# A hybrid decoder layer: router weights loaded earlier, and half of the output projection of two token tiles placed around the last head sums

## The chip, the cores and the metric

The kernel runs on one core of a Trainium2 chip. The core has four compute engines that work side by side and meet at semaphores: TensorE (PE in the profile), VectorE (DVE), ScalarE (ACT) and GpSimd (POOL). A fifth, SyncE (SP), only issues DMA transfers here. The metric is the time of one execution on the device in microseconds (us); the shown time is the median of three runs.

## What is computed

One layer over 1024 tokens with 1024 features, all in float32:

```python
h = rmsnorm(x, ln1_g)
p = h @ w_in                                  # columns shared out to two kinds of heads
oA = stick_breaking_attention(q, k, v)        # 8 heads of 64, features 0..511
oB = gla_chunked(q, k, v, log_a)              # 4 heads, 128 values each, features 512..1023
oB = rmsnorm(oB per head, gla_norm_g) * silu(g_r)
x1 = x + concat(oA, oB) @ w_out
h2 = rmsnorm(x1, ln2_g)
logits = h2 @ [w_group, w_expert] + [b_group, b_expert]    # 4 + 32 columns
y  = x1 + top-2 experts of the best group, each (silu(h2 @ gate) * (h2 @ up)) @ down
out = rmsnorm(y, ln_f_g)
```

Every large product is made exact to float32 by splitting both factors into a high part (float32r, written by ACT) and the rest (written by DVE): three matmuls, high x high, rest x high and high x rest.

## The kernel before

The program is a row of blocks; within a block each engine has its own list of instructions, in an order written by hand, and at the end of a block all engines meet. The blocks are: norm and transposition of x, stick-breaking attention, linear attention (`linear_attention`, L661), output projection and routing (`mix_and_route`, L1362), the experts, and the combination. TensorE's products write to eight banks of PSUM (`bank(k, i)`), and each engine that reads a bank frees it for the next product.

**Linear attention** works on two pairs of heads, p = 0 and 1. TensorE's list interleaves twenty projections `project(n)` (24 matmuls of 512 columns each, L1171) with the seven levels of each pair's scores (`level(g)`, L1247, small matmuls in plain float32). DVE puts a level's result into the score tile with `place_level(g)` (L1027). For pair 1, `turn_v(1)` (L1187) transposes the values, token tiles two at a time, n = 0 to 3, into banks 2 and 3 by turns; so n = 2 waits until DVE's `take_v(1)` (L940) has copied n = 0 away, and in DVE's list `take_v(1)` stands behind `place_level(7)`. In TensorE's list it stands behind `level(7)`.

The pair ends so: `level(12)`, `level(13)`, then `outputs(1)` (L1260, L1265), which needs every level placed; DVE's `gate_out(1)` (L1036) reads the output from banks 0 to 3 and ACT squares it; `sums(1, h)` (L1274) adds the squares over a head's 128 features by a matmul with ones, into banks 4 to 7; ACT takes logarithm and exponential (L835, L839), DVE multiplies (`normed`, L1043), and the block ends. Meanwhile the rows of `w_out` arrive and are split by ACT (L846) and DVE (`split_wo(kd)`, L1047), one of eight row blocks kd at a time, in the space that the projections have left. The features 0 to 511 of the concatenation, `cat[:, 0:4]`, come from stick-breaking and are complete long before. So for token tile 0 their half of the output projection, 24 matmuls (L1326), stands at the end of this block, behind the sums, into banks 0 and 1. DVE's `split_wo(0)` and `split_wo(1)` stand ahead of `place_level(12)` and `place_level(13)`.

**Output projection and routing** goes over eight token tiles t. On TensorE: two column halves of 24 matmuls (L1773), 12 each for t = 0, whose first half is done; between the halves the eight transpositions of tile t - 1 (`turn`, L1743); behind them the router's product of tile t - 1 (`score`, L1753). A tile's matmuls wait for its split parts (`in_hi`, ACT L1539; `in_lo`, DVE L1664). DVE adds x to the product (L1671, tile `cat`), ACT squares and takes the root (L1545, L1549), DVE inverts (L1636), normalizes (L1650), splits the tile after next, and copies the transposed tile (L1629) for the router. Both lists are in strict order.

SP's list in this block begins with two tiles of x and `g2`, then the router's gains, weights and biases (L1445 to L1449: `g2c`, `wr`, `rb`), then a blank list to DRAM (`slots`, L1451), then the first expert's gate and up weights, four transfers of 1024 KB (L1456). DVE waits for all six small loads at t = 0, ahead of the splitting of tile 1, and multiplies the router's weights by the gains (L1660).

Of the kernel before, what the change touches and what calls it, by code (L numbers as in the profile page):

```python
# [99 lines left out]
def _build(nc, ctx, a):  # L100
# [51 lines left out]
    with ExitStack() as c0:  # L152
# [11 lines left out]
        with ExitStack() as front:  # L164
# [6 lines left out]
            w.update(w2=sb("w2", [P, KW], F32, front), gb=sb("gb", [P, GLA_PAIRS], F32, front),  # L171
                     gn=sb("gn", [P, GLA_HEADS], F32, front), small=sem("g_small"))
            with ExitStack() as c2:
                norm_and_turn(k, c2, h_hi, h_lo, cat, w)
            with ExitStack() as c2:
                stick_breaking(k, c2, h_hi, h_lo, cat, w)
            with ExitStack() as c2:
                linear_attention(k, c2, h_hi, h_lo, cat, w, wo)
        passing[0] = False
        gf, gf_in = sb("gf", [P, D], F32, c0), sem("c_gf")  # L180
        with ExitStack() as c:
            tiles = expert_tiles(k, c, cat, raw, high, lower)
            with ExitStack() as c2:
                tables = mix_and_route(k, c2, c, cat, in_parts, tiles, wo, retire)
            x1_in = experts(k, c, tables, tiles, cat, in_parts, gf, gf_in)
# [475 lines left out]
def linear_attention(k, c, h_hi, h_lo, cat, w, wo):  # L661
# [47 lines left out]
    def sum_banks(p, h):  # L709
        return ps[:, 4 * p + 2 * h:4 * p + 2 * h + 2, :]  # L710
# [7 lines left out]
    with nc.Block() as block:  # L718
        @block.sync
        def _(sp):  # L720
            for t in range(first + 2, LAST):
                sp.wait_ge(lo_done, t - 2)
                sp.dma_start(w_raw[:, t % 3], w_dram[:, :, TILE_COLS[t]:TILE_COLS[t] + P]).then_inc(w_in_s[t % 3], 16)
            sp.wait_ge(lo_done, LAST)
# [48 lines left out]
        def _(act):  # L773
# [131 lines left out]
            act.activation(w_hi[:, 0, 0:SB_PAIRS], cat[:, 0:SB_PAIRS, 0:P], ACT.Copy).then_inc(cathi, 1)  # L905
# [13 lines left out]
        def _(dve):  # L919
# [15 lines left out]
            def take_v(p):  # L935
                if p:
                    dve.wait_ge(o_ready, p)
                for n in range(4):
# [128 lines left out]
            take_v(0)  # L1067
# [42 lines left out]
            exponents(9)  # L1110
            place_level(7)
            take_v(1)
# [37 lines left out]
        def _(pe):  # L1150
# [24 lines left out]
            def turn_v(p):  # L1175
                pe.wait_ge(out_done, 16 if p else 4)
# [4 lines left out]
                for n in range(4):  # L1181
# [94 lines left out]

            pe.wait_ge(small, 48)
# [6 lines left out]
            turn_v(0)  # L1284
# [16 lines left out]
            project(15)  # L1301
            level(7)
            turn_v(1)
# [14 lines left out]
            outputs(1)  # L1318
            for h in range(2):
                sums(1, h)  # L1320
            pe.wait_ge(catlo, 1)
            pe.wait_ge(wolo, SB_PAIRS)
            for hf in range(2):
                for kd in range(SB_PAIRS):
                    for m, (x_, w_) in enumerate(((w_hi, wo_hi), (w_lo, wo_hi), (w_hi, wo_lo))):
                        pe.matmul(bank(k, hf), x_[:, 0, kd, :], w_[kd][:, hf * HALF:(hf + 1) * HALF],  # L1326
                                  start=(kd == 0 and m == 0), stop=False)
# [36 lines left out]
def mix_and_route(k, c, out_c, cat, cat_parts, tiles, wo, retire):  # L1364
# [17 lines left out]
    g2c = sb("g2c", [P, KD], F32, c)  # L1382
    x1T = sb("x1T", [P, KD, P], F32, c)
    wr = sb("wr", [P, KD, LOGITS], F32, c)
    rb = sb("rb", [P, LOGITS], F32, c)
# [44 lines left out]

    def x1(t):
# [6 lines left out]
    with nc.Block(no_gpsimd_drain=True) as block:  # L1438
        @block.sync
        def _(sp):  # L1440
# [3 lines left out]
            with nc.allow_non_contiguous_dma(reason="a thousand gains, features to partitions"):  # L1444
                sp.dma_start(g2c[:], a["ln2_g"][0].rearrange("(k p) -> p k", p=P)).then_inc(small, 16)  # L1445
# [814 lines left out]
```

## Time and profile before

| | |
|---|---|
| median of 3 runs | 1294.22 us (1292.25 to 1297.98) |
| the profiled execution | 1290.5 us |
| its span, first to last instruction | 1288.9 us |
| TensorE busy / VectorE / ScalarE / GpSimd | 93% / 70% / 57% / 24% |
| linear attention | to 516.6 us of the span |
| output projection and routing | from there; the first expert matmul starts at 663.7 us |
| experts and combination | the rest |

All places in the text are microseconds from the start of the span. A row of a timeline gives the start of an instruction (or of a merged run of equal ones), its duration, the engine and the line, what is written and read, and in brackets how long the engine was idle before it and who ended that wait. TensorE's matmuls overlap in the pipeline, so that the start of the next one tells more than the end of the last. The granted clock is 1.00 at 2.4 GHz and 0.50 at 1.2 GHz.

### The profile page before, as it was taken

What the parts mean: (1) busy time and instruction counts of PE and PEld (TensorE: products, weight loads), DVE (VectorE), ACT (ScalarE), POOL (GpSimd) and SP (SyncE); (2) the same over time, 40 slices, a digit from 0 to 9 for tenths busy, and PEclk for the clock granted to TensorE, in tenths of its full rate; (3) what the DMA queues carried; (4) which work ended last, traced back from release to release, by engine and by line L of the source; (5) the groups of instructions that cost most, each with busy time, mean ns of one, the idle gap of its engine ahead of it and who ended that gap; (6) DMA issues with size and microseconds to landing.
All of it is one profiled execution on the core that took longest, in us unless ns stands there. A gap on an engine that the chain in (4) does not pass through costs nothing. (4 is left out here: it accounts for less than half of the span.)

```text
span 1288.9 us, 18150 instructions
## 1 busy us (share of the span) xinstructions
PE 1193.2 (93%) x6596; PEld 903.0 (70%) x6596; DVE 902.0 (70%) x844; ACT 739.0 (57%) x760; POOL 307.7 (24%) x273
## 2 busy tenths in 40 slices
PE   3999999999999998799649999999999999999975
PEld 2777777877788786688536777777777777777742
DVE  3366656565475476344759989988989989899725
ACT  5365556464442426211428788777787777887613
POOL 1000000000211010100442444455444454444400
PEclk8999999999999998899869999999999999999988
DMA  5210101000210021833169999999999999999757
GB/s 179 66 34 17 34 18 34 18 17 1 71 45 17 1 99 33 273 126 98 61 239 405 395 382 386 381 388 386 383 380 384 383 387 386 381 386 385 281 198 293
DMA packets 83152, 271.63 MB, mean 211 GB/s; under 512 B 14640, under 2 KB 45472, under 8 KB 58528
## 3 DMA queue, kind: packets, MB, share of 16 engines
q1 hardware_dynamic: 72640, 248.31, 51.7%
q0 software_dynamic: 9312, 18.45, 4.4%
q10 hardware_dynamic: 1152, 4.19, 0.8%
q8 instruction: 34, 0.56, 0.2%
q14 instruction: 14, 0.11, 0.0%
HBM read 253.91 MB, written 25.79 MB: 217 GB/s over the span
## 5 line engine op out<-in xcount | busy, mean ns | idle before, releaser
L2089 PE MATMUL ps<-w_high,in_hi 128*96 128x512 f32 x512 | 204.1, 399 | 4.8 <-DVE hid L2017 2.9
L2089 PE MATMUL ps<-w_lower,in_hi 128*96 128x512 f32 x512 | 202.3, 395 | 0.0
L2089 PE MATMUL ps<-w_high,in_lo 128*96 128x512 f32 x512 | 201.8, 394 | 0.0
L1359 POOL DMA_INDIRECT x_g<-h_dram,who x33 | 157.8, 4781 | 39.7 <-POOL who L1355 27.8
L2031 DVE TENSOR_TENSOR d_lo<-cat,d_hi 128x2048 fp32r<-128x2048 f32 x64 | 146.2, 2286 | 24.6 <-ACT d_hi L1953 24.6
L2003 DVE TENSOR_TENSOR w_lower<-w_raw,w_high 128x2048 fp32r<-128x2048 f32 x62 | 141.7, 2285 | 24.6 <-ACT w_high L1932 24.6
L2008 DVE TENSOR_TENSOR w_lower<-w_raw,w_high 128x2048 fp32r<-128x2048 f32 x64 | 143.4, 2279 | 4.0 <-PEq L1438 4.0
L1938 ACT ACTIVATE w_high<-w_raw 128x2048 fp32r<-128x2048 f32 x62 | 118.9, 1919 | 24.3 <-PE ps L2089 24.3
L1953 ACT ACTIVATE d_hi<-cat 128x2048 fp32r<-128x2048 f32 x64 | 122.3, 1912 | 16.5 <-PEq L1438 13.6
L1932 ACT ACTIVATE w_high<-w_raw 128x2048 fp32r<-128x2048 f32 x62 | 118.2, 1907 | 0.0
L510 DVE TENSOR_TENSOR_SCAN prod<-cat 128x256 f32<-128x256 f32 (+7 forms) x64 | 83.4, 1344 | 41.7 <-ACT cat L438 41.6
L2089 PEld LDWEIGHTS ps<-w_high,in_hi 128*96 128x96 f32 x512 | 83.4, 163 | 38.7 <-DVE w_lower L2003 3.4
L2089 PEld LDWEIGHTS ps<-w_lower,in_hi 128*96 128x96 f32 x512 | 83.2, 163 | 35.6
L2089 PEld LDWEIGHTS ps<-w_high,in_lo 128*96 128x96 f32 x512 | 83.5, 163 | 33.2 <-issue 0.8
L1874 POOL DMA_INDIRECT y_dram<-y,where x32 | 36.2, 1132 | 272.5 <-ACT y L1963 272.5
L577 PE MATMUL ps<-w_high,in_hi 128*128 128x512 f32 x232 | 93.9, 405 | 1.4 <-PEq L213 1.4
L577 PE MATMUL ps<-w_lower,in_hi 128*128 128x512 f32 x232 | 92.5, 399 | 0.0
L577 PE MATMUL ps<-w_high,in_lo 128*128 128x512 f32 x232 | 92.0, 396 | 0.0
L2116 PE MATMUL ps<-d_hi,hT_hi 128*96 128x512 f32 x256 | 81.0, 398 | 1.6 <-DVE hT_lo L2026 1.5
L2116 PE MATMUL ps<-d_lo,hT_hi 128*96 128x512 f32 x256 | 80.3, 395 | 0.0
L2116 PE MATMUL ps<-d_hi,hT_lo 128*96 128x512 f32 x256 | 80.3, 395 | 0.0
L742 POOL MEMSET kl<- 128x2048 f32 x1 | 1.8, 1804 | 281.7 <-POOLq L376 281.7
(315 smaller groups left out, 2382.4 us busy)
## 6 DMA issues: line engine op xcount, KB each, us to landing
w_raw<-exp_w_gate SPq DMA_DIRECT2D x64, 1024.0 KB, 10.1
w_raw<-exp_w_up SPq DMA_DIRECT2D x64, 1024.0 KB, 11.6
cat<-exp_w_down SPq DMA_DIRECT2D x64, 1024.0 KB, 10.8
w_raw<-w_in SPq DMA_DIRECT2D x22, 512.0 KB, 3.8
xt<-x SPq DMA_DIRECT2D x8, 512.0 KB, 6.8
w_raw<-w_out SPq DMA_DIRECT2D x8, 512.0 KB, 5.1
x_g<-x SPq DMA_DIRECT2D x8, 512.0 KB, 3.7
x_dram<-cat SPq DMA_DIRECT2D x8, 512.0 KB, 4.9
```

Of the source, the lines that this page charges most:

```text
L510: dve.tensor_tensor_scan(prod[:, h, T - nk:T][:, ::-1], x, x, 1.0, ALU.mult, ALU.bypass)\
L577: mm = pe.matmul(out, w[:, t % 2, x // 3, :], h[:, x // 3, cols], start=(x == 0), stop=(x == 3 * KD - 1))
L1359: pool.indirect_dma_start(x_g[0:CAP, j, :], None, k["h2_dram"][:, :], bass.IndirectOffsetOnAxis(ap=who[j][0:CAP, 0:1], axis=0), bounds_che ...
L1874: pool.indirect_dma_start(k["y2_dram"][:, :], bass.IndirectOffsetOnAxis(ap=where[j][0:CAP, 0:1], axis=0), y[j][0:CAP, :], None, bounds_che ...
L1932: act.activation(g_hi[:, 4 * m:4 * m + 4], w_g[:, 4 * m:4 * m + 4], ACT.Copy).then_inc(ghi, 1)
L1938: act.activation(u_hi[:, 4 * m:4 * m + 4], w_u[:, 4 * m:4 * m + 4], ACT.Copy).then_inc(uhi, 1)
L1953: act.activation(d_hi[:, part], w_d[j][:, part], ACT.Copy).then_inc(dhi, 1)
L2003: dve.tensor_tensor(g_lo[:, part], w_g[:, part], g_hi[:, part].bitcast(F32), ALU.subtract).then_inc(glo, 1)
L2008: dve.tensor_tensor(u_lo[:, part], w_u[:, part], u_hi[:, part].bitcast(F32), ALU.subtract).then_inc(ulo, 1)
L2031: dve.tensor_tensor(d_lo[:, part], w_d[j][:, part], d_hi[:, part].bitcast(F32), ALU.subtract).then_inc(dlo, 1)
L2089: mm = pe.matmul(out, x_[:, n // 3, :], w_[:, n // 3, :], start=(n == 0), stop=(n == 3 * KD - 1))
L2116: mm = pe.matmul(ps[0:CAP, 2 + m, :], x_[:, f, :], w_[:, f, cols], start=(f == 0 and n == 0), stop=(f == KF - 1 and n == 2))
```

## The change

- The five router loads leave SP's list in `mix_and_route` and go into SP's list in `linear_attention`, behind the load of the sixth weight tile (t = first + 5). Their tiles live from there on, with a semaphore of their own. DVE's multiplication of the router's weights moves behind the addition of x at t = 0; `normalize(0)` gets a wait for `g2`.
- `turn_v(1)` and `take_v(1)` are cut in two. The first half (n = 0, 1) goes ahead of `level(7)` on TensorE and ahead of `place_level(7)` on DVE.
- DVE does `place_level(12)` first, then `split_wo(0)`, then `place_level(13)`, then `split_wo(1)` to `(3)`.
- The first half of the output projection is made for two token tiles: tile 0 into banks 4 and 5 between `outputs(1)` and `sums(1, h)`, tile 1 into banks 2 and 3 behind the sums. The sums go to banks 6, 7 and 0, 1. ACT and DVE split `cat[:, 0:4]` for both tiles. In `mix_and_route` tile 1 then has 24 matmuls instead of 48, and its split there covers the features 512 to 1023 only.

```diff
@@ linear_attention
     def sum_banks(p, h):
-        return ps[:, 4 * p + 2 * h:4 * p + 2 * h + 2, :]
+        first_bank = ((0, 2), (6, 0))[p][h]
+        return ps[:, first_bank:first_bank + 2, :]
@@ SP
                 sp.dma_start(w_raw[:, t % 3], w_dram[:, :, TILE_COLS[t]:TILE_COLS[t] + P]).then_inc(w_in_s[t % 3], 16)
+                if t == first + 5:
+                    with nc.allow_non_contiguous_dma(reason="a thousand gains, features to partitions"):
+                        sp.dma_start(g2c[:], a["ln2_g"][0].rearrange("(k p) -> p k", p=P)).then_inc(router_in, 16)
+                    sp.dma_start(wr[:, :, 0:GROUPS], a["w_group"][0].rearrange("(k p) n -> p k n", p=P)).then_inc(router_in, 16)
...
@@ ACT
-            act.activation(w_hi[:, 0, 0:SB_PAIRS], cat[:, 0:SB_PAIRS, 0:P], ACT.Copy).then_inc(cathi, 1)
+            for t in range(2):
+                act.activation(w_hi[:, t, 0:SB_PAIRS], cat[:, 0:SB_PAIRS, t * P:(t + 1) * P], ACT.Copy).then_inc(cathi, 1)
@@ DVE
             exponents(9)
+            take_v(1, 0, 2)
             place_level(7)
-            take_v(1)
+            take_v(1, 2, 4)
...
-            for kd in range(2):
+            place_level(12)
+            split_wo(0)
+            place_level(13)
+            for kd in range(1, SB_PAIRS):
                 split_wo(kd)
-            place_level(12)
-            place_level(13)
-            for kd in range(2, SB_PAIRS):
-                split_wo(kd)
-            dve.wait_ge(cathi, 1)
-            dve.tensor_tensor(w_lo[:, 0, 0:SB_PAIRS], cat[:, 0:SB_PAIRS, 0:P], w_hi[:, 0, 0:SB_PAIRS].bitcast(F32),
-                              ALU.subtract).then_inc(catlo, 1)
+            for t in range(2):
+                dve.wait_ge(cathi, t + 1)
+                dve.tensor_tensor(w_lo[:, t, 0:SB_PAIRS], cat[:, 0:SB_PAIRS, t * P:(t + 1) * P],
+                                  w_hi[:, t, 0:SB_PAIRS].bitcast(F32), ALU.subtract).then_inc(catlo, 1)
@@ PE
-            def turn_v(p):
-                pe.wait_ge(out_done, 16 if p else 4)
+            def turn_v(p, first, last):
+                pe.wait_ge(out_done, (16 if last == 4 else 15) if p else 4)
...
             project(15)
+            turn_v(1, 0, 2)
             level(7)
-            turn_v(1)
+            turn_v(1, 2, 4)
...
             outputs(1)
+            mix_first_half(0, 4)
             for h in range(2):
                 sums(1, h)
...
+            mix_first_half(1, 2)
@@ mix_and_route, DVE
-                if t == 0:
-                    dve.wait_ge(small, 96)
-                    dve.tensor_tensor(wr[:], wr[:], over(g2c[:], [P, KD, LOGITS]), ALU.mult).then_inc(ready, 1)
...
                 if t >= 1:
                     score(t - 1)
+                if t == 0:
+                    dve.wait_ge(router_in, 80)
+                    dve.tensor_tensor(wr[:], wr[:], over(g2c[:], [P, KD, LOGITS]), ALU.mult).then_inc(ready, 1)
                 if 0 <= t < NT - 1:
                     invert(t)
                     normalize(t)
@@ mix_and_route, PE
-                    n = 0 if t else 3 * SB_PAIRS
+                    n = 0 if t > 1 else 3 * SB_PAIRS
-                    for kd in range(0 if t else SB_PAIRS, KD if t < NT else 0):
+                    for kd in range(0 if t > 1 else SB_PAIRS, KD if t < NT else 0):
```

The new `mix_first_half(t, at)` waits for the split of tile t and for the rests of `w_out`'s first four row blocks, then issues the 24 matmuls that stood at L1326, into `bank(k, at + hf)`.

## Rows read from the trace of the kernel before

**Rows 1.** Timeline of PE, 445 to 452 us: start, duration, instruction, [idle before].

```profile
444.97 2.00 PE L1247 MATMUL ps<-ql,kl 64*128 64x64 f32 x32
446.90 1.09 PE L1187 MATMUL ps<-ident,cat 128*128 128x128 f32 x8
450.07 1.25 PE L1187 MATMUL ps<-ident,cat 128*128 128x128 f32 x8 [2.07 <-DVE gv L940]
451.07 0.47 PE L1171 MATMUL ps<-w_high,in_hi 128*128 128x512 f32 x1
```

**Rows 2.** Timeline of DVE at the same place.

```profile
447.02 2.47 DVE L1027 COPY_PREDICATED s_all<-masks,ps 128x512 f32<-128x512 int32 x2 [12.41 <-PE ps L1247]
```

**Rows 3.** Stretches: length, busy PE, PEld, DVE, ACT, POOL (x); clock; DMA share, GB/s.

```profile
452.00:491.40 39.40, 39.40 (x354) 34.01 (x352) 28.29 (x42) 10.27 (x14) 5.40 (x5) 1.00 0.30 108
...
492.90:499.60 6.70, 5.14 (x24) 5.14 (x25) 6.52 (x8) 6.67 (x7) 0.00 (x0) 0.50 0.00 0
...
506.60:509.80 3.20, 3.20 (x5) 1.35 (x4) 3.06 (x3) 1.11 (x1) 0.00 (x0) 0.50 0.00 0
510.00:515.90 5.90, 5.90 (x26) 4.50 (x24) 1.69 (x2) 4.41 (x4) 0.00 (x0) 1.00 0.00 0
...
527.10:533.70 6.60, 5.39 (x13) 4.23 (x14) 3.74 (x5) 3.67 (x5) 0.61 (x1) 0.50 1.01 376
...
700.00:1240.00 540.00, 537.75 (x2538) 387.02 (x2537) 476.07 (x299) 412.77 (x297) 240.80 (x178) 1.00 0.98 374
```

**Rows 4.** Timeline of PE: the first pair's outputs and second sum.

```profile
424.98 3.73 PE L1260 MATMUL ps<-s_all,gv 128*128 128x128 f32 x32
...
437.71 1.88 PE L1274 MATMUL ps<-b_all,ones 128*128 128x512 f32 x4
```

**Rows 5.** Timeline of PE, 487 to 545 us.

```profile
487.71 3.79 PE L1247 MATMUL ps<-ql,kl 64*128 64x64 f32 x64
494.46 6.31 PE L1260 MATMUL ps<-s_all,gv 128*128 128x128 f32 x32 [2.96 <-DVE s_all L1027]
...
505.18 5.40 PE L1274 MATMUL ps<-e,ones 128*128 128x512 f32 x8 [2.65 <-DVE cat L1036]
...
518.34 0.50 PE L1773 MATMUL ps<-w_high,in_hi 128*128 128x512 f32 x1 [2.30 <-DVE in_lo L1664]
...
528.31 0.80 PE L1773 MATMUL ps<-w_high,in_hi 128*128 128x512 f32 x1 [4.24 <-DVE in_lo L1664]
...
542.79 1.87 PE L1753 MATMUL ps<-wr,x1T 128*128 128x36 f32 x16
544.49 0.48 PE L1773 MATMUL ps<-w_high,in_hi 128*128 128x512 f32 x1
```

**Rows 6.** Timeline of DVE: placing and splitting around 490 us.

```profile
489.39 2.36 DVE L1047 TENSOR_TENSOR w_lower<-w_raw,w_high 128x1024 fp32r<-128x1024 f32 x2 [2.98 <-ACT w_high L846]
491.67 2.74 DVE L1027 COPY_PREDICATED s_all<-masks,ps 128x512 f32<-128x512 int32 x4
```

**Rows 7.** Timeline of DVE in the output projection, tiles 0 and 1.

```profile
526.67 0.46 DVE L1660 TENSOR_TENSOR wr<-wr,g2c 128x288 f32<-128x288 f32 x1 [8.38 <-DMA rb<-b_expert]
...
528.18 1.22 DVE L1671 TENSOR_TENSOR cat<-ps,x_g 128x1024 f32<-128x1024 f32 x1
...
534.33 1.22 DVE L1664 TENSOR_TENSOR in_lo<-cat,in_hi 128x1024 fp32r<-128x1024 f32 x1
537.07 1.29 DVE L1629 COPY x1T<-ps 128x512 f32<-128x512 f32 x2 [1.53 <-PE ps L1743]
```

**Rows 8.** Timeline of SP: weight tiles, router loads, blank list.

```profile
343.09 9.63 SPq L723 DMA_DIRECT2D w_raw<-w_in  x2
...
518.17 0.43 SPq L1445 DMA_DIRECT2D g2c<-ln_g  x1
...
524.24 0.43 SPq L1451 DMA_DIRECT2D slots<-h  x1
```

**Rows 9.** DMA issues, 516 to 530 us: KB, us to landing.

```profile
slots<-h SPq DMA_DIRECT2D x1, 576.0 KB, 3.8
```

More of the change, by code:

```diff
@@ L176, in _build @@
                 stick_breaking(k, c2, h_hi, h_lo, cat, w)
+            router = (sb("wr", [P, KD, LOGITS], F32, c0), sb("rb", [P, LOGITS], F32, c0), sb("g2c", [P, KD], F32, c0),
+                      nc.alloc_semaphore(name="router_in"))
             with ExitStack() as c2:
-                linear_attention(k, c2, h_hi, h_lo, cat, w, wo)
+                linear_attention(k, c2, h_hi, h_lo, cat, w, wo, router)
         passing[0] = False
@@ L183, in _build @@
             with ExitStack() as c2:
-                tables = mix_and_route(k, c2, c, cat, in_parts, tiles, wo, retire)
+                tables = mix_and_route(k, c2, c, cat, in_parts, tiles, wo, router, retire)
             x1_in = experts(k, c, tables, tiles, cat, in_parts, gf, gf_in)
@@ L657, in _, with linear_attention @@
                     turn_v(p)
-def linear_attention(k, c, h_hi, h_lo, cat, w, wo):
+def linear_attention(k, c, h_hi, h_lo, cat, w, wo, router):
     nc, sb, sem, ps, a, ident, ones, V, A, G = (
@@ L720, in _ @@
         def _(sp):
+            wr, rb, g2c, router_in = router
             for t in range(first + 2, LAST):
@@ L933, in gate_1, with take_v @@
                 dve.tensor_tensor(gate_place(1, h), gate_place(1, h), b_all[:, h], ALU.mult).then_inc(r_done, 1)
-            def take_v(p):
+            def take_v(p, first, last):
                 if p:
                     dve.wait_ge(o_ready, p)
-                for n in range(4):
+                for n in range(first, last):
                     dve.wait_ge(vturn, 4 * p + n + 1)
@@ L1066, in _ @@
             split_lo(first + 3)
-            take_v(0)
+            take_v(0, 0, 4)
             decayed(0)
@@ L1180, in turn_v @@
                     pe.wait_ge(x_done, 4)
-                for n in range(4):
+                for n in range(first, last):
                     if p and n >= 2:
@@ L1275, in sums, with mix_first_half @@
                 mm.then_inc(summed, 1)
+            def mix_first_half(t, at):
+                pe.wait_ge(catlo, t + 1)
+                pe.wait_ge(wolo, SB_PAIRS)
+                for hf in range(2):
+                    for kd in range(SB_PAIRS):
+                        for m, (x_, w_) in enumerate(((w_hi, wo_hi), (w_lo, wo_hi), (w_hi, wo_lo))):
+                            pe.matmul(bank(k, at + hf), x_[:, t, kd, :], w_[kd][:, hf * HALF:(hf + 1) * HALF],
+                                      start=(kd == 0 and m == 0), stop=False)
             pe.wait_ge(small, 48)
@@ L1361, in gather_rows, with mix_and_route @@
                             bounds_check=T - 1, oob_is_err=False).then_inc(gathered[j], 16)
-def mix_and_route(k, c, out_c, cat, cat_parts, tiles, wo, retire):
+def mix_and_route(k, c, out_c, cat, cat_parts, tiles, wo, router, retire):
     nc, sb, sem, ps, a, ident, ones, V, G = (k[n] for n in ("nc", "sb", "sem", "ps", "a", "ident", "ones", "V", "G"))
@@ L1381, in mix_and_route @@
     g2 = sb("g2", [P, D], F32, c)
[L1382 removed]
     x1T = sb("x1T", [P, KD, P], F32, c)
[L1384 to L1385 removed]
+    wr, rb, g2c, router_in = router
     logits = sb("logits", [P, NT, LOGITS], F32, c)
@@ L1647, in normalize @@
                     dve.wait_ge(blanked, 16)
+                    dve.wait_ge(small, 16)
                 if t >= 2:
@@ L1772, in _ @@
                         for x_, w_ in ((cat_hi, wo_hi), (cat_lo, wo_hi), (cat_hi, wo_lo)):
-                            mm = pe.matmul(bank(k, 2 * j + hf), x_[:, j, kd, :], w_[kd][:, cols], start=(n == 0),
+                            mm = pe.matmul(bank(k, mix_bank(t, hf)), x_[:, j, kd, :], w_[kd][:, cols], start=(n == 0),
                                            stop=(n == 3 * KD - 1))
```

33 lines of the change are left out of this document (14 added, 19 removed).

## The prediction, made before the change was built

> **What bounds the kernel now.** I read the page first. TensorE is busy nearly all the time, and the slices where it is not lie at the start, around 500 to 540 us, in the routing and at the end; in the same slices its granted clock falls. The experts, more than 500 us, are full: TensorE works 537.75 of 540 us, with the DMA engines at a share of 0.98 [rows 3]. Nothing of the change lies in there, so what is won ahead of them should arrive at the end as it is. Then I read TensorE's timeline from the last projections to tile 2, and for each idle time the timeline of the engine named in its bracket.
>
> From 452 to 491.4 us TensorE is never idle, while VectorE works 28.3 and ScalarE 10.3 of those 39.4 us [rows 3]: there TensorE is the limit. Ahead of it is an idle time of 2.07 us, in which it waits for VectorE to copy the turned values [rows 1]; VectorE is late with that only since its list has `place_level(7)` first, which waits 12.41 us for TensorE [rows 2]. Behind it TensorE waits four times: 2.96 us for the last placing, 2.65 us for the gated outputs, 2.30 us at the border of the blocks, 4.24 us for the split of tile 1 [rows 5]. The last one comes from the router's loads: VectorE stood 8.38 us waiting for them, with the split behind that wait [rows 7]. Three of these idle times are followed or accompanied by a granted clock of 0.50, that is 1.2 GHz: 492.9 to 499.6, 506.6 to 509.8 and 527.1 to 533.7 us [rows 3].
>
> **The values' transposition in two parts.** From `level(7)` to `project(16)` TensorE takes 451.07 - 444.97 = 6.10 us [rows 1]. With two turns ahead of the level, two behind, no wait is left: 1.93 us of level (446.90 - 444.97) and twice 1.09 us of turns make 4.1 us. What the first turns need from ScalarE and VectorE is there by then: VectorE is idle until 447.02 [rows 2] and copies n = 0 and 1 while the level runs. Moved instructions: sixteen matmuls and two copies, none more than before. **Gain 2.0 us**, if VectorE does not hold TensorE later; its `place_level(7)` now comes 1.0 us later, its copies are then partly done, and it has 11 us of idle time in the 39.4 that follow [rows 3]. The ends of this term are 0 and 2.3.
>
> **Placing level 12 first.** TensorE's last two levels now run from 487.71 - 2.0 = 485.7 to 489.5 us (3.79 us, [rows 5]); the first of them ends halfway, at 487.6. VectorE places it (a placing is half of 2.74 us, [rows 6]) by 489.0, does `split_wo(0)` (half of 2.36, [rows 6]) by 490.2, and places level 13 by 491.6. The outputs start there instead of at 494.46: 2.86 us, of which 2.0 are the term above. **Gain 0.85 us.** TensorE's idle time ahead of the outputs shrinks from 2.96 to 2.1 us. The three splits left and the two small ones of `cat` (half as wide, 0.6 each) end at about 496.4 and two gate products at about 498.8. Nobody waits for them until the outputs are done.
>
> **The outputs** took 505.18 - 2.65 - 494.46 = 8.07 us at the low clock [rows 5]. At the full clock the first pair's main part took 3.73 us instead of 6.31 [rows 4, 5]; with that the outputs would take 5.5. I take 8.07, since what stands ahead is the same small matmuls and an idle time nearly as long; the clock fell before, when about 1.4 us of that idle time had passed (491.5 to 492.9, [rows 3, 5]). The low end of this term is -2.5 us, the upper is nothing. The outputs end at 499.7.
>
> **Tile 0's half ahead of the sums.** Before, 2.65 us of waiting and 5.40 us of sums followed the outputs, 8.05 us. Now 24 matmuls at 0.227 us (26 in 5.90, [rows 3]) and 0.3 for the first, 5.75 us, and then the sums. VectorE gates the outputs meanwhile (502.3), so the sums wait for TensorE only. Dense matmuls stand ahead of them, so I price them at the full clock: the first pair's second sum took 1.88 us [rows 4], two take some 3.6 us as they overlap. Together 9.35 us. **Loss 1.3 us** on the path to the block's end. If the low clock went on for all 24 (13 took 5.39 us, [rows 3]: 0.41 each) it would be 4.5 us more.
>
> **Tile 1's half behind the sums.** From the end of the sums (510.58) to tile 0's first matmul (518.34) there are 7.76 us [rows 5] of ScalarE, VectorE and the meeting of the engines; the change leaves them. Tile 1's 24 matmuls, 5.75 us, lie under them, where tile 0's lay. Cost nothing; without that cover, 5.75 us. The sums' other banks need no new wait on this path. The idle time at the border stays near 2.3 us.
>
> **Tile 1 in the output projection.** Tile 0's second half is as before, 5.74 us. From its end, 524.08, to tile 2's first matmul, 544.49, it was 20.4 us [rows 5]: 4.24 of waiting, 14.5 of tile 1 with the turns, 1.7 of the router's product. Now tile 1 has 24 matmuls: 5.45 and 1.1 for turns and starts, 6.6 us. But another wait becomes the last: the router's product of tile 0 needs the copies of the turned tile, and these stand in VectorE's list behind the addition, the inverse root, the normalization and the split of tile 2. From the end of the addition (529.40) to that of the split (535.55) it was 6.15 us, and the copies take 1.29 [rows 7]. With 0.1 and 1.22 for the addition and 0.05 to TensorE, 8.8 us from the end of tile 0; TensorE is done after 6.6, waits 2.2, and tile 2 starts after 8.8 + 1.7 = 10.5 us. **Gain 9.9 us.** The router's multiplication (0.46 us, [rows 7]) lies between addition and inverse, where VectorE waits for ScalarE's square and root; uncovered it costs 0.46. From tile 2 on nothing changes.
>
> **The loads.** In the earlier block SP issues the router's five loads in 524.24 - 518.17 = 6.1 us [rows 8] behind a weight tile issued at 343.09; the next one went out at about 352.4 [rows 8], so some 3 us are to spare. Price nothing; if they were late, that load has its own matmuls two projections off. In the later block the blank list and the four expert loads go out 6.1 us earlier. VectorE needs the list at `normalize(0)`. It is issued 1.8 us into the block, lands 3.8 us later [rows 9], and the normalization starts some 12 us into the block.
>
> **The sum.** 2.0 + 0.85 - 1.3 + 9.9 = 11.45 us. Against it stands the clock in the new idle time of 2.2 us ahead of the router's product. Idle times of 2.07 and 2.30 us left the clock at 1.00, those of 2.65 and 2.96 did not [rows 1, 3, 5]. Here small matmuls of 36 columns follow the idle time, as it was with small ones around 492, so I take a fall of the shortest length seen, 3.3 us [rows 3]. It covers some eight dense matmuls at 0.41 instead of 0.227: 1.5 us (ends 0 and 2.4). The change gives **9.9 us**: 1290.5 - 9.9 = 1280.6 for the profiled execution, whose span of 1288.9 lies 1.6 below its time. The median of the runs is 3.7 above the profiled one, so 1294.2 - 9.9 = **1284.3 us**.
>
> **Rivals.** (a) *The clock stays up.* Ahead of the outputs and ahead of the router's product every idle time is now shorter than each after which a fall was seen. Then the outputs take 2.5 us less and the 1.5 us fall away: gain 13.9, 1280.3 us. Against it speaks that the fall at 492.9 came within the idle time, not at its end. The Trainium skill, page "TensorE: Matmul & The Clock Gate", section "Why this matters for your kernels", warns only of idle gaps between bursts longer than any left here; by it this rival would be the forecast. The trace does not agree: 2.65 us was enough at 506.6 [rows 3, 5]. Chance 0.15.
> (b) *VectorE eats the front's gain.* It is only a few tenths of a microsecond earlier behind `take_v`, and if a later level waits for a placing, the 2.0 us are gone: 1286.3 us. For it: VectorE's idle times in the stretch may all be waits for TensorE. Against it: TensorE waits for nothing there. Chance 0.12.
> (c) *The experts' weights get in the way.* Four times 1024 KB at 376 GB/s [rows 3] are 11 us of traffic, now right behind the blank list and x. If the list landed behind them, after 15 us instead of 3.8, the normalization would be 5 us late: gain 4.9, 1289.4 us. Before, they stood just as close behind the list and it took 3.8 us [rows 9]. The Trainium skill, page "DMA: Bandwidth & Descriptors", section on HWDGE ordering, says that a later transfer of one issuing engine may finish before an earlier one; no row here shows it. Chance 0.10.
> (d) *The filling does not fill.* The low clock goes on under tile 0's half, 4.5 us more on the path: gain 5.4, 1288.9 us. Chance 0.09.
> (e) *Slower.* In the experts both TensorE and the DMA engines are full [rows 3], and where the loop starts against the stream of weights is changed. If the weights' rate became the limit, each per cent of it costs 5.4 us; from 374 x (1 - 9.9 / 540) = 367 GB/s on the whole gain is gone, and with 3% less the time is 1284.3 + 16.2 = 1300.5 us. Against it: TensorE waits 2.25 us in 540 now, and the loop's order is untouched. Chance 0.04.
> The forecast has the other 0.50.
>
> **How the numbers follow.** Some 0.5%, 6.5 us, is what a measurement of this kernel can tell from no change. The forecast, (a) and (b) are faster by more, together 0.77; (b) is near the border, which leaves 0.76. (c), (d) and that remainder are within 0.5%, 0.20; (e) is slower, 0.04. The range reaches from a little below (a) to a little above (c), 1279 to 1290, with the runs' own spread of some 2 us taken in, and leaves out (e) and the far ends of the others.
>
> **What would show it.** In the changed kernel's profile: no idle time inside the turns, `project(16)` some 4.1 us behind `level(7)`'s place; 2.1 us of waiting ahead of the outputs; the 24 matmuls right behind the outputs and no wait at the sums; tile 1's half ended before VectorE's last product of the block; VectorE not waiting for the router's loads; tile 1 in 6.6 us and a wait of about 2.2 us ahead of the first router product, tile 2 starting near 533 us. Wrong would be the prediction if a wait grew between 452 and 490 us, if the sums waited for `cat`'s split, if `normalize(0)` waited for DMA, or if the experts took more than their time now.

## The result and the profile after

The changed kernel takes **1283.26 us** (median of 4 runs, 1281.59 to 1284.75), the kernel before, timed beside it, 1295.5 (1292.25 to 1297.98). The ratio is 0.991, with a 95% interval of 0.9881 to 0.9939: some 11.7 us less. The forecast was 1284.3 with a range of 1279 to 1290. In a second series, six runs against nineteen, the ratio was 0.9921 (0.9899 to 0.9943), some 10.2 us less. The two profiled executions lie closer together than the medians, 1290.5 and 1284.75 us with spans of 1288.9 and 1283.2; the last part of this section says why.

Timeline of TensorE in the changed kernel, at the turns of the values; the lines answer to [rows 1]:

```profile
444.76 1.03 PE L1203 MATMUL ps<-ident,cat 128*128 128x128 f32 x8
445.73 2.00 PE L1263 MATMUL ps<-ql,kl 64*128 64x64 f32 x32
447.66 1.09 PE L1203 MATMUL ps<-ident,cat 128*128 128x128 f32 x8
448.51 0.48 PE L1187 MATMUL ps<-w_high,in_hi 128*128 128x512 f32 x1
```

No row has a bracket: the idle 2.07 us are gone, and the piece takes 448.51 - 444.76 = 3.75 us instead of 6.10.

Timeline of TensorE from the outputs to tile 3, answering to [rows 5]; L1276 and L1281 are the outputs, L1290 the sums, L1771 the router's product, L1791 the output projection:

```profile
490.95 6.73 PE L1276 MATMUL ps<-s_all,gv 128*128 128x128 f32 x32 [2.00 <-DVE s_all L1042]
497.61 1.83 PE L1281 MATMUL ps<-vT,k_dec 64*128 64x128 f32 x28
504.97 3.60 PE L1290 MATMUL ps<-e,ones 128*128 128x512 f32 x8
516.34 0.50 PE L1791 MATMUL ps<-w_high,in_hi 128*128 128x512 f32 x1 [2.32 <-DVE in_lo L1679]
...
517.66 0.63 PE L1791 MATMUL ps<-w_lower,in_hi 128*128 128x512 f32 x1
...
520.64 0.53 PE L1791 MATMUL ps<-w_high,in_hi 128*128 128x512 f32 x1
...
532.41 1.98 PE L1771 MATMUL ps<-wr,x1T 128*128 128x36 f32 x16 [2.40 <-DVE x1T L1646]
534.22 0.48 PE L1791 MATMUL ps<-w_high,in_hi 128*128 128x512 f32 x1
...
549.42 0.48 PE L1791 MATMUL ps<-w_high,in_hi 128*128 128x512 f32 x1
```

The sums have no bracket any more; tile 0's half stands between L1281 and L1290 (499.37 to 504.97). The wait of 4.24 us ahead of tile 1 is gone, and a wait of 2.40 us ahead of the first router product has come, for VectorE's copies. Tile 2 starts 10.3 us earlier than before (534.22 against 544.49), tile 3, at 549.42 against 558.07, only 8.65.

Where the clock is low (columns as in [rows 3]):

```profile
491.00:497.80 6.80, 6.80 (x34) 6.68 (x36) 6.74 (x7) 6.77 (x7) 0.00 (x0) 0.56 0.00 0
517.50:520.80 3.30, 3.30 (x10) 2.52 (x9) 0.00 (x0) 0.00 (x0) 0.60 (x6) 0.50 0.75 235
534.60:537.90 3.30, 3.30 (x10) 2.54 (x9) 2.91 (x4) 1.32 (x3) 0.51 (x1) 0.50 1.09 402
700.00:1240.00 540.00, 534.92 (x2525) 384.26 (x2523) 472.94 (x297) 413.41 (x297) 233.76 (x179) 1.00 0.98 371
```

One fall at the outputs, as before (it lasts from 490.3 to 497.0 us, so that the first row begins inside it and ends behind it); one behind the border of the blocks, which the profile before did not have; and one in tile 2, behind the new wait. The (x10) of such a row also counts the matmuls that its ends cut. By their starts, the seven dense matmuls from 517.66 to 520.64 take 2.98 us instead of the 1.59 of seven at 0.227. The experts stand as they stood: DMA share 0.98, 371 GB/s against 374.

VectorE in the changed kernel, from the addition at tile 0 to the one at tile 1, answering to [rows 7]:

```profile
523.77 1.22 DVE L1686 TENSOR_TENSOR cat<-ps,x_g 128x1024 f32<-128x1024 f32 x1 [6.89 <-PE ps L1791]
524.91 0.45 DVE L1692 TENSOR_TENSOR wr<-wr,g2c 128x288 f32<-128x288 f32 x1
527.82 0.17 DVE L1653 RECIPROCAL o_inv<-o_rms 128x1 f32<-128x1 f32 x1 [2.46 <-ACT o_rms L1566]
528.02 2.09 DVE L1668 SCALAR_TENSOR_TENSOR h<-cat,o_inv,g 128x1024 f32<-128x1024 f32 x1
529.95 1.22 DVE L1679 TENSOR_TENSOR in_lo<-cat,in_hi 128x1024 fp32r<-128x1024 f32 x1
531.07 1.29 DVE L1646 COPY x1T<-ps 128x512 f32<-128x512 f32 x2
```

The router's multiplication lies in the wait for ScalarE's root, as forecast, and the copies come last, right ahead of the router's product.

**Between tile 3 and the experts** the profile loses 4.3 of the 8.65 us: the first expert matmul starts at 659.38 against 663.71. Of the small steps that choose the experts of the last two tiles, VectorE in the changed kernel:

```profile
630.84 0.19 DVE L1618 TENSOR_TENSOR run<-run,am 128x32 f32<-128x32 f32 x1
632.09 0.19 DVE L1620 TENSOR_TENSOR run<-run,am 128x32 f32<-128x32 f32 x1 [1.06 <-issue]
632.81 0.16 DVE L1625 TENSOR_REDUCE gsum<-e 128x2 f32<-128x8 f32 x1 [0.52 <-DVE run L1620]
633.40 0.16 DVE L1626 SCALAR_TENSOR_TENSOR den<-e,gsum 128x2 f32<-128x2 f32 x1 [0.43 <-DVE gsum L1625]
634.80 0.17 DVE L1627 RECIPROCAL rows<-den 128x2 f32<-128x2 f32 x1 [1.24 <-DVE den L1626]
```

VectorE stands idle between steps that wait for nothing but each other. I call these idle times the halts in the routing. From the start of the last router product to that of the last cast of slot numbers it is 622.45 to 636.49, 14.0 us, where the first profile of before had 631.03 to 640.66, 9.6. The experiments come back to this.

### The profile page after: what moved, and what is told of

It reads as the page before. It is cut to its first block and busy times, and to the rows that moved or that the text cites. A ratio compares the mean times of both kernels' runs of the same rounds, so it can differ in the third digit from the quotient of the medians.

```text
span 1283.2 us, 18157 instructions
## 1 busy us (share of the span) xinstructions
PE 1193.8 (93%) x6596; PEld 904.2 (70%) x6596; DVE 902.4 (70%) x845; ACT 740.5 (58%) x761; POOL 301.7 (24%) x273
## 5 line engine op out<-in xcount | busy, mean ns | idle before, releaser
L1380 POOL DMA_INDIRECT x_g<-h_dram,who x33 | 151.5, 4590 | 40.4 <-POOL who L1376 27.7
```

What stands on the lines that cost most here:

```text
L1380: pool.indirect_dma_start(x_g[0:CAP, j, :], None, k["h2_dram"][:, :], bass.IndirectOffsetOnAxis(ap=who[j][0:CAP, 0:1], axis=0), bounds_che ...
```

## The experiments

Theory: the forecast's steps, each gain in its place. Rivals: the clock makes the difference; parts of the change do not add; the halts in the routing belong to the change. The experiments were timed in three series. Kernels are compared by their ratio to the kernel before, timed in the same series, since the latter's median differed from one series to the next (1293.24, 1289.66 and 1288.15 us). The changed kernel itself was timed only in the first of the three (ratio 0.9921); a difference between its ratio and one of the later series is uncertain by some 4 us, and is called a gain below only where traces or kernels of one series bear it out. A piece of the trace that serves as a measure is the way from the start of the outputs to the first matmul of tile 3: 58.5 and 57.2 us in the two profiles of the changed kernel, 63.6 in the first profile of the kernel before and 61.4 in its second, which comes below.

**The changed kernel again.** No edit.

> The changed kernel once more, unchanged. Both theories: the gain over the kernel before is 9 to 12 us on the median. Its first profile lost 3.3 us in the routing of the last two tiles, where VectorE stood between its own small steps (6.5 us from the pair masks to the slot numbers instead of 3.2). If that belongs to the change, it is there again; if it is an accident of one execution, the stretch takes 3.2 us as before and the span is near 1280.

1283.47 us, ratio 0.9921, 10.2 us less than the kernel before, as both theories had it. The span was 1281.4. The halts were there again: 619.26 to 633.36, 14.1 us. But the outputs ran at the full clock: from 489.07 to tile 0's half at 494.60, 5.53 us instead of 8.42, after the same idle time:

```profile
489.07 3.17 PE L1276 MATMUL ps<-s_all,gv 128*128 128x128 f32 x26 [2.02 <-DVE s_all L1042]
...
527.61 2.74 PE L1771 MATMUL ps<-wr,x1T 128*128 128x36 f32 x16 [2.40 <-DVE x1T L1646]
530.16 0.77 PE L1791 MATMUL ps<-w_high,in_hi 128*128 128x512 f32 x1
530.73 0.63 PE L1791 MATMUL ps<-w_high,in_lo 128*128 128x512 f32 x1
```

One and the same program thus gives 2.9 us more or less at this place. Behind the router's product the low clock was there again, and twice as long (528.7 to 535.3): tile 2 took 546.24 - 530.16 = 16.1 us, an undisturbed tile 13.6.

**The router's loads alone**, on the kernel before:

```diff
                 sp.dma_start(w_raw[:, t % 3], w_dram[:, :, TILE_COLS[t]:TILE_COLS[t] + P]).then_inc(w_in_s[t % 3], 16)
+                if t == first + 5:
+                    ...
-                if t == 0:
-                    dve.wait_ge(small, 96)
-                    dve.tensor_tensor(wr[:], wr[:], over(g2c[:], [P, KD, LOGITS]), ALU.mult).then_inc(ready, 1)
```

> The kernel before with the router's five loads moved into linear attention, and nothing else. Theory (the loads were the last wait ahead of tile 1): TensorE's 4.24 us ahead of tile 1 go, the low clock from 527 to 534 with them (2.4 us), tile 2 starts 6.6 us earlier, near 537.9 us; total 6 to 7 us less. Rival (another load or the blank list is as late): 0 to 2 us.

1286.59 us, ratio 0.994 (0.9919 to 0.9961), 7.7 us less. From the start of tile 0 TensorE goes through tiles 0 and 1 without a wait, and tile 2 starts at 537.57, 0.3 us from the expected place:

```profile
516.89 0.57 PE L1779 MATMUL ps<-w_high,in_hi 128*128 128x512 f32 x1 [2.29 <-DVE in_lo L1667]
...
535.87 1.87 PE L1759 MATMUL ps<-wr,x1T 128*128 128x36 f32 x16
537.57 0.48 PE L1779 MATMUL ps<-w_high,in_hi 128*128 128x512 f32 x1
```

That it is so close is luck in part. Tile 0 already starts 1.45 us earlier than in the first profile of before (516.89 against 518.34), since the sums ran at the full clock (3.70 us instead of 5.40), and from tile 0 to tile 2 the gain is 26.15 - 20.68 = 5.5 us, not 6.6, since the clock fell behind the border.

By the ratios of this series it is three quarters of the whole gain (10.2 us) from the simplest part. The wait for the loads was a real one, and no other wait took its place here.

**The turns in two parts alone**, on the kernel before (with `take_v(1)` in two parts on VectorE):

```diff
+            turn_v(1, 0, 2)
             level(7)
-            turn_v(1)
+            turn_v(1, 2, 4)
```

> The kernel before with the second pair's value transposition in two parts, and nothing else. Theory: level 7 and the turns take 3.8 to 4.1 us instead of 6.1, level 12 starts 2.0 to 2.5 us earlier, and tile 2 too; total 2.0 to 2.5 us less. Rival (VectorE holds TensorE later): level 12 starts at 487.7 as before, total 0.

1291.75 us, ratio 0.998 (0.9965 to 0.9994), 2.6 us less. The piece takes 3.75 us (444.66 to 448.41), and the last levels start at 485.02 instead of 487.71. VectorE held nothing later in this profile, which speaks against rival (b).

**The router's loads put back** into the changed kernel (the five loads stand in SP's list of the later block again; the cut shows VectorE's part):

```diff
...
+                if t == 0:
+                    dve.wait_ge(router_in, 80)
+                    dve.tensor_tensor(wr[:], wr[:], over(g2c[:], [P, KD, LOGITS]), ALU.mult).then_inc(ready, 1)
                 if t + 1 < NT:
                     dve.wait_ge(cathi, t + 2)
...
```

> The changed kernel with the router's loads back in the output projection's block and VectorE's wait for them back ahead of tile 1's split. Theory: VectorE stands some 8.4 us for the last load, tile 1 waits 3 to 4 us, and the first router product comes as much later: tile 2 starts 3 to 5 us later than in the changed kernel, total 3 to 5 us more. Rival (tile 1's early half has made room for the wait): under 1 us more.

1284.19 us, ratio 0.9918 (0.9889 to 0.9947): no difference from the changed kernel, 0.9921. The theory's number fell. VectorE does stand 9.15 us for the loads, and TensorE waits for it:

```profile
525.31 0.46 DVE L1677 TENSOR_TENSOR wr<-wr,g2c 128x288 f32<-128x288 f32 x1 [9.15 <-DMA rb<-b_expert]
```

```profile
516.21 0.80 PE L1790 MATMUL ps<-w_high,in_hi 128*128 128x512 f32 x1 [2.32 <-DVE in_lo L1681]
526.43 0.79 PE L1790 MATMUL ps<-w_high,in_hi 128*128 128x512 f32 x1 [3.01 <-DVE in_lo L1681]
...
534.92 1.98 PE L1770 MATMUL ps<-wr,x1T 128*128 128x36 f32 x16 [0.40 <-DVE x1T L1645]
536.72 0.48 PE L1790 MATMUL ps<-w_high,in_hi 128*128 128x512 f32 x1
```

But 3.01 us at tile 1 take the place of 2.00 of the 2.40 us ahead of the router's product, and the low clock that followed the latter moves with the wait: tile 2 takes 13.6 us (550.31 - 536.72). From the outputs to tile 3 it is 58.1 us, against 58.5 and 57.2 in the two profiles of the changed kernel. The loads' move is worth 7.7 us without the early halves and nothing measurable with them: 3 us more are not excluded by the timing, but the 58.1 us speak against them. The parts of this change do not add.

**The kernel before again.** No edit.

> The kernel before once more, unchanged. In the routing of the last two tiles (from the last router product to the second cast of slot numbers) its first profile took 9.6 us, the changed kernel and three single edits 14.0 to 15.0 us. Theory (VectorE's short halts there come to every kernel of this family, and the first profile of before escaped them): 13.5 to 15 us here too. Rival (the edits cause them): 9.6 us again.

One execution, 1287.33 us. TensorE's last router product and VectorE's last cast:

```profile
627.27 2.74 PE L1753 MATMUL ps<-wr,x1T 128*128 128x36 f32 x16 [1.01 <-DVE x1T L1629]
```

```profile
637.60 0.17 DVE L1622 CAST slot<-slot_f 128x4 uint32<-128x4 f32 x1
```

The stretch took 10.3 us: the theory's number fell. The two early profiles of the changed kernel and three more of single edits had 14.0 to 15.0 us, this one and the seven kernels still to come 9.5 to 11.0, among them some that differ from the changed kernel by one line. The rival, that the edits cause the halts, is not borne out either: two kernels below that keep the moved loads, the turns and the placing (the halves as before the change, and VectorE's list altered) were short, 9.6 and 10.9 us, and the whole changed kernel with ten matmuls added had 10.0.

What goes with the halts is the chip. The four long profiles of the first series ran on one chip; this one and the seven still to come ran on two others, and none of the eight was long. (For the first profiles of before and after the chip is not on record.) The kernel before has no profile from the chip of the long ones, but its median there was 3.6 to 5.1 us above those on the other two, about what the halts cost. So the chip is the nearest explanation, and this run, on another chip, could not test whether the kernel before has the halts too. No run separates the chip from the time of the series, and the cause stays open.

The profile of before that stood ahead of the prediction was a short one and the first of after a long one, which hid about 4 us of the gain between them.

This second profile also shows how much the first one varies by the clock: the sums took 3.70 us instead of 5.40, at the full clock behind the same wait of 2.65 us, the clock fell behind the border, and the wait ahead of tile 1 was 2.81 us instead of 4.24. Tile 3 starts at 554.31 here and at 546.24 in the changed kernel's second profile, 8.1 us apart, where the first two had 8.65.

**Both halves behind the sums:**

```diff
-            mix_first_half(0, 4)
             for h in range(2):
                 sums(1, h)
+            mix_first_half(0, 4)
             mix_first_half(1, 2)
```

> The changed kernel with both tiles' halves behind the sums. Theory: TensorE waits 2.65 us for the gated outputs again, and 48 matmuls (11.1 us) behind the sums are longer than the 6 us of logarithms, roots and products that they lie under, so the block ends with TensorE; from the start of the outputs to tile 0's first matmul 27.5 to 30 us instead of 25.4 (22.5 at the full clock), total 2 to 4 us more. Rival (a half ahead of the sums only delays them): the same or 1.3 us less.

1283.89 us beside 1289.66, ratio 0.9952 (0.9933 to 0.997): some 4 us more than the changed kernel, just beyond the uncertainty of the two ratios. TensorE:

```profile
490.66 3.84 PE L1276 MATMUL ps<-s_all,gv 128*128 128x128 f32 x32 [2.02 <-DVE s_all L1042]
...
500.48 6.42 PE L1290 MATMUL ps<-e,ones 128*128 128x512 f32 x8 [4.22 <-DVE cat L1051]
...
519.55 0.50 PE L1791 MATMUL ps<-w_high,in_hi 128*128 128x512 f32 x1 [1.75 <-DVE in_lo L1679]
```

From the outputs to tile 0 it is 28.9 us, within the expected 27.5 to 30. To tile 3 it is 60.4 us, 1.9 and 3.2 more than in the changed kernel. The first row shows the outputs at the full clock, yet the wait for the gated outputs is then 4.22 us instead of 2.65: VectorE is not ready earlier because TensorE is.

**Tile 1's half in the output projection again**, tile 0's still ahead of the sums:

```diff
...
-            mix_first_half(1, 2)
...
-                    for kd in range(0 if t > 1 else SB_PAIRS, KD if t < NT else 0):
+                    for kd in range(0 if t > 0 else SB_PAIRS, KD if t < NT else 0):
```

> The changed kernel with tile 1's half made in the output projection again, tile 0's half still between outputs and sums. Theory: TensorE has 48 matmuls for tile 1 and no wait ahead of the first router product; from tile 0's first matmul to tile 2's 19.4 us instead of 16.3 without and 17.9 to 18.6 with the low clock; total 1 to 3 us more. Rival (the whole early half is worth its 5.45 us): 5 us more.

1280.2 us, ratio 0.9923 (0.9903 to 0.9942), as the changed kernel:

```profile
514.44 0.80 PE L1790 MATMUL ps<-w_high,in_hi 128*128 128x512 f32 x1 [7.76 <-DVE in_lo L1678]
```

TensorE waits 7.76 us at the border, with nothing to do, and from tile 0 (514.44) to tile 2 (535.59) it is 21.15 us, 3.3 and 2.5 more than in the changed kernel's two profiles. The expected 19.4 was 1.75 too low, mainly since the clock stayed low for 6.7 us around the end of that wait (512.1 to 518.8). Tile 2 then takes 13.6 us instead of 15.2 and 16.1, since no wait and no low clock stand ahead of it. From tile 0 to tile 3 it is then 34.75 us, against 33.1 and 34.7. The expected 1 to 3 us more are neither seen nor excluded by the timing; the rival's 5 us are excluded.

**The halves as before the change**, with the other parts kept:

```diff
-            mix_first_half(0, 4)
             for h in range(2):
                 sums(1, h)
+            mix_first_half(0, 4)
```

(and tile 1's half in the output projection, as above)

> The changed kernel with the output projection's halves as they were before the change: tile 0's behind the sums, tile 1's in the output projection; router loads, transpositions in two parts and the placing order stay as changed. Theory (the rearranged halves bring nothing by themselves: 5.6 us ahead of the sums in place of a wait of 2.65 to 4.2, given back at tile 1): at the full clock the way from the outputs to tile 3 is 52.4 us in both; total within 1.5 us of the changed kernel. Rival (the halves are worth what the forecast gave them, 3 us or more): 3 us or more above the changed kernel.

1278.45 us beside 1288.15, ratio 0.9924 (0.9896 to 0.9952): the changed kernel without its rearranged halves is as fast as with them.

```profile
488.96 3.84 PE L1276 MATMUL ps<-s_all,gv 128*128 128x128 f32 x32 [2.00 <-DVE s_all L1042]
```

From the outputs (488.96) to tile 3 (545.46) it is 56.5 us, against 58.5 and 57.2 in the changed kernel. The expected 52.4 us held in none of them, since each had low clocks on the way. The two ratios by themselves do not exclude the rival's 3 us. But a kernel of this same series, the changed one with two matmuls of no use (the experiment after the next), took 1279.69 us, 1.2 more than this one and not 3 less, and the traces say the same.

**The new wait filled:** ten matmuls of no use ahead of the first router product.

```diff
+                if t == 1:
+                    for n in range(10):
+                        pe.matmul(bank(k, 7), wo_hi[n % KD][:, 0:P], wo_hi[n % KD][:, 0:HALF], start=True, stop=True)
                 if t >= 1:
                     score(t - 1)
```

> The changed kernel with ten matmuls of no use (512 columns each, 2.27 us) in TensorE's wait ahead of the first router product. Theory (the wait lets the clock fall): the granted clock stays at 1.00 through tile 2, whose first 24 matmuls take 5.6 us instead of 7.2 to 8.0; the router product starts as before; total 1.5 to 2.5 us less. Rival (the fall comes from the router product or from elsewhere): the low clock is there as before, total 0.

1276.46 us beside 1289.66, ratio 0.9895 (0.987 to 0.9919), 3.3 us less than the changed kernel by the ratios, which alone would not be clear of their uncertainty. TensorE, and its clock from there to tile 3:

```profile
527.38 2.43 PE L1798 MATMUL ps<-w_high 128*128 128x512 f32 x10
529.96 1.98 PE L1771 MATMUL ps<-wr,x1T 128*128 128x36 f32 x16
531.76 0.48 PE L1791 MATMUL ps<-w_high,in_hi 128*128 128x512 f32 x1
```

```profile
527.30:531.80 4.50, 4.36 (x29) 3.58 (x27) 3.73 (x5) 0.73 (x1) 0.53 (x1) 1.00 1.00 411
531.80:545.30 13.50, 13.50 (x74) 11.52 (x73) 6.10 (x7) 1.76 (x5) 1.01 (x2) 1.00 0.55 198
```

The router's product starts where it would have started (16.0 us behind tile 0, 16.1 in the changed kernel), and tile 2 takes 13.6 us. The work is of no use, so the gain is the clock's: 1.6 and 2.5 us in the traces. The router's product is there in every kernel. With the wait of 2.4 us ahead of it the clock fell in four profiles of four; without the wait, or with it filled or cut to 0.40 us, tile 2 took 13.6 us in the ten others. That the cause of this fall is the wait is shown.

**The wait ahead of the outputs filled:**

```diff
+            def filler():
+                pe.wait_ge(state_done, (NT - 1) * 2)
+                for hf in range(2):
+                    pe.matmul(bank(k, 2 + hf), ones[:], e[:, 1, hf * HALF:(hf + 1) * HALF], start=True, stop=True)
...
+            filler()
             outputs(1)
```

> The changed kernel with two matmuls of no use (float32, 512 columns, 1.7 us) in TensorE's wait ahead of the second pair's outputs. Theory (the wait behind the small matmuls of the levels lets the clock fall): outputs 5.5 us in every profile instead of 8.4, total 1 to 2.5 us less. Rival: the small matmuls alone let it fall; outputs near 8 us, total 0.

1279.69 us, ratio 0.9932 (0.9906 to 0.9959), as the changed kernel. Its outputs took 5.5 us, but so they did in most profiles without the filling: of eight without a filling, with an idle time of 2.0 us ahead of the outputs, three had the low clock there (8.42, 8.27 and, in part, 7.06 us), of four with 2.96 us all four. The last experiment, with the same filling, had the full clock too, and two of two against five of eight decides nothing on this fall.

**VectorE's list altered**, the version that the new wait calls for:

```diff
+                if t == 1:
+                    normalize(0)
-                if t >= 1:
+                if t >= 2:
                     take_turned(t - 1)
...
+                if t == 0:
+                    take_turned(0)
                 if 0 <= t < NT - 1:
                     invert(t)
-                    normalize(t)
+                    if t:
+                        normalize(t)
```

> The changed kernel with VectorE's list altered at tiles 0 and 1: the copies of turned tile 0 come ahead of the inverse root, and the normalization of tile 0 behind the split of tile 2. Theory (the forecast's new last wait is VectorE's list): TensorE's 2.4 us ahead of the first router product go, with them the low clock in tile 2; from tile 0's first matmul to tile 2's 14.0 us instead of 16.3 to 18.6; total 3.5 to 4.5 us less than the changed kernel. Rival (tile 2's split becomes the last): 1 us less.

1273.83 us beside 1288.15, ratio 0.9895 (0.987 to 0.9921): 3.4 us less than the changed kernel by the ratios, 13.5 less than the kernel before (14.3 by the medians). The difference of the ratios is within their uncertainty, but two kernels of this one series differ by nothing but VectorE's list, the one above with the filling (1278.87 to 1280.62 us) and the last one below (1272.6 to 1277.19): 4.6 us between the medians. VectorE and TensorE:

```profile
522.39 1.29 DVE L1646 COPY x1T<-ps 128x512 f32<-128x512 f32 x2 [1.50 <-PE ps L1766]
523.59 0.15 DVE L1653 RECIPROCAL o_inv<-o_rms 128x1 f32<-128x1 f32 x1
524.37 1.23 DVE L1679 TENSOR_TENSOR in_lo<-cat,in_hi 128x1024 fp32r<-128x1024 f32 x1 [0.62 <-ACT in_hi L1556]
525.51 2.02 DVE L1668 SCALAR_TENSOR_TENSOR h<-cat,o_inv,g 128x1024 f32<-128x1024 f32 x1
```

```profile
525.38 1.87 PE L1776 MATMUL ps<-wr,x1T 128*128 128x36 f32 x16
527.08 0.48 PE L1796 MATMUL ps<-w_high,in_hi 128*128 128x512 f32 x1
```

The copies now come while VectorE would wait for the root, the router's product has no bracket, and from tile 0 (511.85) to tile 2 it is 15.2 us: 1.2 more than expected, which is the low clock behind the border (511.9 to 515.3).

**Both**, VectorE's altered list and the filling ahead of the outputs.

> Both: VectorE's altered list and the two matmuls of no use ahead of the outputs. Theory: the two gains add, 5 to 6.5 us less than the changed kernel, 15 to 17 us less than the one before. Rival (the clock falls somewhere else instead): no better than the altered list alone.

1275.05 us, ratio 0.9891 (0.987 to 0.9911), as the altered list alone. The gains do not add: the filling brings nothing that can be measured. The outputs took 5.53 us both here and with the altered list alone, so in the profiles there was no fall for it to prevent.

## Why the prediction was right, and where its steps were not

**The turns.** Forecast 4.1 us for the piece and a gain of 2.0; measured 3.75 and 2.35. The small difference is turns of 0.97 and 0.85 us in place of 1.09. Alone it gave 2.6 us (0.8 to 4.5) in the timing.

**Placing.** The idle time ahead of the outputs was forecast at 2.1 us and measured 2.00; the outputs start at 490.95 instead of the forecast 491.6. No run has the placing alone; the idle times give it 0.96 us where 0.85 was forecast.

**The outputs.** I took the low clock's 8.07 us, and the first profile had 8.42; but in five of eight profiles with this shorter wait there was no fall. Here rival (a) was more often right than the forecast. It matters in the changed kernel, where tile 0's half follows the outputs at once: from the outputs to tile 0 it was 22.5 us with the full clock and 25.4 with the low one. Where the sums follow the outputs, their wait for VectorE grows by part of what the outputs save (4.22 and 3.72 us instead of 2.65).

**Tile 0's half and the sums.** Forecast 5.75 and 3.6 + 7.76 us; measured 5.60 (499.37 to 504.97) and 11.37 (504.97 to 516.34). Both terms hit. The loss of 1.3 us was a different matter: it set them against sums of 5.40 us at a low clock, and in the second profile of before, and in that of the loads alone, the same sums took 3.70. Against those the loss is 3.0 us.

**The border.** Forecast: 2.3 us idle as before, and the clock kept, since it was kept in [rows 5]. The idle time was 2.32 us, but the clock fell, here and in nine later profiles with 2.3 us at the border; only the first profile of before and that of the turns alone kept it. That single row was the exception, and the step that read it as a rule failed. Tile 0's second half took 7.33 us (516.34 to 523.67) instead of 5.74, 1.6 us more. The second profile of the kernel before had this fall as well. That the idle time causes it is not shown, since no run fills it. With 1.75 us at the border, in the kernel with both halves behind the sums, the clock stayed up, in one profile.

**Tile 1 and the new wait.** The chain was right in kind and in length: 10.5 us forecast from the end of tile 0 to tile 2, 534.22 - 523.77 + 0.1 = 10.55 measured; the wait 2.2 against 2.40; the fall behind it as forecast, and 1.6 us by tile 2's 15.2 us against 13.6. The filled wait and the altered list show from two sides that the wait came from the order of VectorE's list and the fall from the wait.

**What the sum hid.** The term of 9.9 us mixed two things. The router's loads alone bring 7.7 us in the timing (5.0 to 10.5 by the interval), and the run with the halves as before shows no gain from the rearranged halves beside them. Counted from the traces at places without a low clock, tile 0's half ahead of the sums takes 5.6 us where a wait of 2.65 stood, 2.95 more; tile 1's half saves 10.9 / 2 = 5.45 us of matmuls, of which VectorE's chain gives back the 2.40 us wait, 3.05 less. The two cancel to about 1 us, since the wait ahead of the sums and the clock differ between profiles. I should have asked not what tile 1 saves against a tile that had waited for the loads, but against one that had not.

**The sum.** Forecast 9.9 us. Measured 8.65 us at tile 3, where the fall at the border took 1.6 us that the forecast did not have; 5.7 us in the spans of the two profiles, because of the halts in the routing; 11.7 and 10.2 us by the ratios, which are not tied to two executions. What these have above the 8.1 and 8.65 us of the traces no row accounts for, and it lies within the intervals. So the time was right because the steps were summed for the change as built; the errors within it (the border, the low clock at the outputs and at the sums) are of 1 to 3 us each and go both ways. Rivals (c), (d) and (e) left no trace: the inverse ahead of `normalize(0)` waits for the root (2.46 us, <-ACT) and `normalize(0)` itself for nothing, tile 0's half takes 5.60 us at the full clock, and the experts start to end in 623.8 us against 625.2.

## What to carry to other kernels

A part of a change is worth what it brings beside the other parts: price each against the kernel that has the others, since two edits that take away the same wait share one gain. When a wait is taken away, read what is queued on the engine behind it; here the next wait lay in the order of VectorE's own list, and moving two of its steps gave 3.4 us by the ratios and 4.6 between two kernels of one series, where the moved matmuls gave nothing measurable. A short wait of TensorE can cost the low clock behind it besides itself, and whether the clock falls differs between executions of one program, so that one profile's row is a sample and not a rule.

## What the runs showed of the hardware

The same program had its outputs at the full and at the low clock after the same idle time of 2.0 us (5.53 and 8.42 us). Of twelve waits of 2.3 us at the border, with dense matmuls on both sides, ten were accompanied or followed by a low clock of some 3.4 us; of waits of 2.4 us ahead of the sparse router product all four, for 3.3 to 3.4 or 6.7 to 6.8 us; of waits of 2.96 us behind the sparse levels all four, for 6.8 us. Of four waits of 2.65 us ahead of the sums two were. The Trainium skill, page "TensorE: Matmul & The Clock Gate", section "Why this matters for your kernels", warns of longer gaps only. The trace does not agree: the filled wait shows that one of 2.4 us costs the low clock too. For the others only the sequence is shown.

VectorE's dependent small steps in the routing took 14.1 to 15.0 us in all four profiles of one series, on one chip, and 9.5 to 11.0 in the eight of two other series on two other chips; the edits do not explain it. The cause stays open.
